# Forget attention: one inverse per query applied to the head's context instead of to every row of probabilities

## The reference

```python
sf = jnp.einsum('bqhd,bkhd->bhqk', qf, fk) * (FOX_HEAD_DIM ** -0.5)
sf = sf + cq[..., :, None] - cum_k[..., None, :]       # running sums of log forget gates
pf = jax.nn.softmax(jnp.where(causal, sf, NEG), axis=-1)
of = jnp.einsum('bhqk,bkhd->bqhd', pf, fv)
...
x = x + rmsnorm(concat([od, of]) @ w_out, ln_attn_post)
```

## Time and profile before

| | |
|---|---|
| median of 3 runs | 1392.2 us (1389.93 to 1393.25) |
| the profiled execution's own time | 1387.27 us |
| its span, first to last instruction | 1385.3 us |
| TensorE, weight load, VectorE, ScalarE busy | 1316.9, 1109.3, 784.4, 555.7 us |
| forget attention | 890.2 to 985.0 us of the span |
| mean granted TensorE clock | 0.983 |

### The profile page before, as it was taken

One profiled execution on the slowest core, in us unless ns is written; L12 is line 12 of the kernel. 1 busy time (PEld: TensorE's weight loads), 2 busy tenths in 40 slices (PEclk: granted clock), 3 DMA queues, 4 the chain that ended last, 5 costly groups with the idle time before them and its releaser, 6 DMA issues.

```text
span 1385.3 us, 17842 instructions
## 1 busy us (share of the span) xinstructions
PE 1316.9 (95%) x6548; PEld 1109.3 (80%) x6548; DVE 784.4 (57%) x1298; ACT 555.7 (40%) x914; POOL 44.9 (3%) x47
## 2 busy tenths in 40 slices
PE   7998879999999999999999999999899999999996
PEld 6877767789888888888777887878798788888886
DVE  5776767556644544222675797586685632355434
ACT  5645545534323223322454654555552322223221
POOL 3000000000000000000021000010000000000002
PEclk9999989999999999999999999999999999999999
DMA  5220110321232233333223232330211232222322
GB/s 177 92 92 16 54 46 16 99 69 61 92 100 97 91 97 113 109 106 106 91 91 107 91 99 84 92 92 31 92 62 61 92 107 91 91 97 100 106 92 76
DMA packets 37101, 120.46 MB, mean 87 GB/s; under 512 B 4508, under 2 KB 6556, under 8 KB 37040
## 3 DMA queue, kind: packets, MB, share of 16 engines
q1 hardware_dynamic: 36464, 117.98, 26.2%
q0 software_dynamic: 576, 1.65, 0.4%
HBM read 112.27 MB, written 2.11 MB: 83 GB/s over the span
## 4 chain that ended last, share of the span: by engine, by line
PE 77%; DVE 14%; ACT 4%; issue 3%; DMA 1%; POOL 0%; POOLq 0%; ACTq 0%; DVEq 0%; SPq 0%
PE bank L779 24%; PE bank L781 24%; PE bank L780 24%; DVE w_lo L1863 3%; DVE tiles L1863 2%; DVE tiles L1866 2%; DVE arena L1863 2%; DVE probsT L1863 1%; PE bank L923 1%; ACT w_hi L1327 1%; PE bank L885 1%; PE bank L876 1%; DVE arena L1866 1%; DVE negmax L2071 1%; ACT arena L1348 1%
## 5 line engine op out<-in xcount | busy, mean ns | idle before, releaser
L1863 DVE TENSOR_TENSOR w_lo<-raw_slab,w_hi 128x1024 fp32r<-128x1024 f32 x199 | 244.3, 1227 | 295.1 <-ACT w_hi L1327 279.7
L779 PE MATMUL bank<-u_hi,w_hi 128*128 128x512 f32 x852 | 337.8, 396 | 14.8 <-DVE tiles L1863 3.8
L781 PE MATMUL bank<-u_hi,w_lo 128*128 128x512 f32 x852 | 334.3, 392 | 0.0
L780 PE MATMUL bank<-u_lo,w_hi 128*128 128x512 f32 x852 | 334.2, 392 | 0.0
L1327 ACT ACTIVATE w_hi<-raw_slab 128x1024 fp32r<-128x1024 f32 x189 | 199.2, 1054 | 183.7 <-PE bank L781 179.9
L779 PE MATMUL bank<-arena,w_hi 128*128 128x512 f32 (+1 forms) x672 | 253.8, 378 | 9.7 <-DVE w_lo L1863 4.9
L780 PE MATMUL bank<-arena,w_hi 128*128 128x512 f32 (+1 forms) x672 | 251.8, 375 | 0.0
L781 PE MATMUL bank<-arena,w_lo 128*128 128x512 f32 (+1 forms) x672 | 251.8, 375 | 0.0
L779 PEld LDWEIGHTS bank<-u_hi,w_hi 128*128 128x128 f32 x852 | 161.2, 189 | 51.7 <-DVE tiles L1863 5.1
L781 PEld LDWEIGHTS bank<-u_hi,w_lo 128*128 128x128 f32 x852 | 161.3, 189 | 34.3
L780 PEld LDWEIGHTS bank<-u_lo,w_hi 128*128 128x128 f32 x852 | 161.4, 189 | 31.8
(11 more groups left out here) (221 smaller groups left out, 1564.7 us busy)
## 6 DMA issues: line engine op xcount, KB each, us to landing
raw_slab<-in_stream SPq DMA_DIRECT2D x207, 512.0 KB, 3.4
arena<-arena SPq DMA_DIRECT2D x32, 128.0 KB, 2.3
residual<-in_xT SPq DMA_DIRECT2D x8, 256.0 KB, 7.8
out_hT<-residual SPq DMA_DIRECT2D x16, 128.0 KB, 1.7
arena<-forget_rows SPq DMA_DIRECT2D x8, 128.0 KB, 2.3
tiles<-in_pT POOLq DMA_DIRECT2D x2, 256.0 KB, 3.0
tiles<-bias_rows POOLq DMA_DIRECT2D x1, 512.0 KB, 3.9
tiles<-in_positions POOLq DMA_DIRECT2D x1, 256.0 KB, 3.5
```

What stands on the lines that cost most here:

```text
L779: pe.matmul(o, ws[0], xs[0], start=first, stop=False)
L780: pe.matmul(o, ws[0], xs[1], start=False, stop=False)
L781: return pe.matmul(o, ws[1], xs[0], start=False, stop=last)
L1863: return nc.vector.tensor_tensor(o, a, b, op)
```

## The change

In forget attention alone, the exponentials go into the transpositions as they are. VectorE takes one inverse of the four row sums of a head at once (`fox_inverse`, at its step 4h+5). TensorE spreads these 512 inverses over the partitions, four 128x128 matmuls against the identity into bank 6 (`fox_factor`, at the end of step 4h+6), and ScalarE copies the head's 64 rows of them to a tile (step 4h+7). When the context is complete, VectorE multiplies it with that tile in place (end of step 4h+9), ScalarE copies the high half from the tile (end of its step 4h+9), and VectorE makes the low half (end of step 4h+10; for the last head in the same step). Bank 6 holds factors, so contexts have bank 5 alone: the next head's context may begin when the product has been made (`fox_scaled`).

```diff
+LAG_FACTOR = LAG_HEAD - 3
-CTX_BANKS = {"ml": (5,), "mla": (5, 6), "df": (5,), "fx": (5, 6)}
+CTX_BANKS = {"ml": (5,), "mla": (5, 6), "df": (5,), "fx": (5,)}
 # plan_psum
+        if a == "fx":
+            for h in range(FX_H):
+                use(("factor", h), 6, (sem.fox_factor, h + 1), (sem.fox_kept, h + 1))
-                free = {"ml": ..., "df": (sem.ctx_scaled, u // ST + 1)}
+                free = {"ml": ..., "df": (sem.ctx_scaled, u // ST + 1), "fx": (sem.fox_scaled, u // ST + 1)}
 # TensorE, attention
-                        pe.wait_ge(sem.probs_ready, UNIT0[a] + v + 1)
+                        if a == "fx":
+                            pe.wait_ge(sem.exp_done, EXP0["fx"] + v + 1)
+                        else:
+                            pe.wait_ge(sem.probs_ready, UNIT0[a] + v + 1)
...
+                    if a == "fx" and at_head("fx", step, LAG_FACTOR) is not None:
+                        fox_factor(at_head("fx", step, LAG_FACTOR))
+            def fox_factor(h):
+                o, e = claim(("factor", h)), EXP0["fx"] + h * ST
+                pe.wait_ge(sem.fox_inverse, h + 1)
+                for i in range(ST):
+                    last = pe.matmul(o[:, i * P:(i + 1) * P], rowinv[:, e + i:e + i + 1].to_broadcast([P, P]), ident, start=True, stop=True)
+                last.then_inc(sem.fox_factor, 1)
 # ScalarE
-            attention("fx", softmax_exp("fx"), plain_head("fx", fx_rows), fx_filled)
+            def fox_head(step):
+                h = at_head("fx", step, LAG_FACTOR + 1)
+                if h is not None:
+                    r, tile = fx_rows(h)
+                    if h:
+                        act.wait_ge(sem.mix_lo, HEAD0["fx"] + h)
+                    nc.scalar.activation(tiles[r, TMP + 1], full(act, ("factor", h))[r, :], ACT.Copy).then_inc(sem.fox_kept, 1)
+                h = at_head("fx", step, LAG_HEAD)
+                if h is not None:
+                    r, tile = fx_rows(h)
+                    act.wait_ge(sem.fox_scaled, h + 1)
+                    nc.scalar.activation(arena[r, MIX_HI + tile], tiles[r, TMP + 1], ACT.Copy).then_inc(sem.mix_hi, 1)
+            attention("fx", softmax_exp("fx"), fox_head, fx_filled)
 # VectorE
+            def fox_inverse(step, units):
+                v = step - LAG_NORM
+                if 0 <= v < units and v % ST == ST - 1:
+                    e = EXP0["fx"] + v + 1 - ST
+                    dve.wait_ge(sem.exp_done, e + ST)
+                    nc.vector.reciprocal(rowinv[:, e:e + ST], rowsum[:, e:e + ST]).then_inc(sem.fox_inverse, 1)
+            def fox_head(step):
+                h = at_head("fx", step, LAG_HEAD)
+                if h is not None:
+                    r, _ = fx_rows(h)
+                    o = full(dve, ("ctx", "fx", h))
+                    dve.wait_ge(sem.fox_kept, h + 1)
+                    tt(tiles[r, TMP + 1], o[r, :], tiles[r, TMP + 1], ALU.mult).then_inc(sem.fox_scaled, 1)
+                if h != FX_H - 1:
+                    h = at_head("fx", step, LAG_HEAD + 1)
+                if h is not None:
+                    r, tile = fx_rows(h)
+                    mix_low("fx", h, r, tile, tiles[r, TMP + 1])
-            attention("fx", softmax("fx", one_softmax("fx")), row_maxima("fx"), plain_head("fx", fx_rows), fx_taken, fx_split)
+            attention("fx", fox_inverse, row_maxima("fx"), fox_head, fx_taken, fx_split)
```

More of the change, by code:

```diff
@@ L312, in attention @@
                 n = HEAD0[a] + u // ST
-                free = {"ml": (sem.sq_done, SQ0.get(f"ml{u // ST}", 0) + 1), "df": (sem.ctx_scaled, u // ST + 1)}
+                free = {"ml": (sem.sq_done, SQ0.get(f"ml{u // ST}", 0) + 1), "df": (sem.ctx_scaled, u // ST + 1), "fx": (sem.fox_scaled, u // ST + 1)}
                 use(("ctx", a, u // ST), CTX_BANKS[a][u // ST % len(CTX_BANKS[a])], (sem.ctx_ready, (UNIT0[a] + u + 1) // 2), free.get(a, (sem.mix_lo, n + 1)))
@@ L516, in __init__ @@
         self.fox_query = new("fox_query")
+        self.fox_inverse = new("fox_inverse")
+        self.fox_factor = new("fox_factor")
+        self.fox_kept = new("fox_kept")
+        self.fox_scaled = new("fox_scaled")
 def build(nc, xT, pT_in, pos_in, cols_in, square_in, onehot_in, relb_in, stream, out):
```

## The result

The changed kernel takes 1395.13 us (median of 7 runs, 1392.46 to 1397.67) against 1389.93 for the kernel before in the same 7 rounds (1388.40 to 1393.25): a ratio of 1.0040, 95% interval 1.0027 to 1.0052, so 3.8 to 7.2 us slower. Forecast were +4.9 us and 1397.1; the kernel before itself came out 2.3 us under the 1392.2 that the forecast started from, so the difference is what to compare. The profiled execution took 1397.67 us, the slowest of its seven, with a span of 1395.9.

The account below looks back on a forecast made before the run. TensorE's work and its standstills bound the kernel. Terms -1.1 +3.0 -0.5 +1.8 -0.6 +0.75 gave +3.4 us, with 1.5 for the clock +4.9: 1392.2 to 1397.1 us, range 1392.0 to 1400.0.

Parts of the forecast that it names:

- up to step 9: Before head 0's context: waits for scaled rows shrink by 1.1, small ones by 0.5, spread adds 0.45; -1.1 us.
- head 0, with the clock: Step 9 and behind: new stall, head 1's spread, one old wait gone, +3.0 us; lower clock behind it, +1.5.
- head 2: The chain after its last maximum takes 6.4 us instead of 5.5, with spread and product wait inside it; +0.9.
- The new wait: Head 1's first product of probabilities and values waits for head 0's context product, behind fq3's split; a stall of +3.2 us.
- The clock: Behind the new stall TensorE's clock falls to about 0.5 for one 3.4 us stretch; +1.5 us, bounds 0 and 4.5.
- The spreads: TensorE's four spreads a head take 0.45 us; seven of eight lie on its path, +3.2 us in all.
- The waits behind VectorE: Heads' TensorE waits on VectorE's product, low halves and splits; for heads 2 and 5, a 6.4 us chain, +1.8 for both.
- The end: After the last context the product precedes both halves, lengthening TensorE's 1.41 us wait by 0.75; the last spread is free.
- Rival 1: Forget attention: the clock holds, all else as forecast; +3.4 us, 1395.6; chance 0.20.
- rival 2: New stalls in forget attention come to 2 or 3 us, the clock stays; 0 to +2, say 1393; chance 0.20.
- Rival 4: ScalarE stands at each head's end for VectorE's product, every head paying 1 us more; +8 to +10, 1401; chance 0.07.
- Rival 3: Transpositions bound by scaling alone, context free in time, idle ahead of the end goes; -4.7 us, 1387.5; chance 0.05.

Follow-up runs that it names:

- e1_product_first: The changed kernel with VectorE's product of context and factors moved ahead to the place of the inverse; 1388.01 us, ratio 0.9987 to the kernel before.
- e2_one_bank_alone: The kernel before with forget attention's contexts in bank 5 alone, rows still scaled, no spreads, no product; ratio 1.0021 to the kernel before.
- e3_busy_in_wait: The changed kernel with 13 unread matmuls just ahead of TensorE's wait for head 0's product; ratio 1.0020 to the kernel before.
- e4_spreads_twice: The changed kernel with each head's four spreads made twice into the same bank; ratio 1.0072 to the kernel before.
- e5_one_spread: e1_product_first with the four spreads for head 0 only, one matmul of one column for each other head; ratio 0.9992 to the kernel before.
- e6_diagonal: e1_product_first with the spread made as one float32 product of ones with a diagonal from GpSimd; ratio 1.0012 to the kernel before.
- e9_diagonal_in_halves: e1_product_first with the last head's product and halves in two parts, and factors from two GpSimd diagonals in float32r; ratio 0.9996 to the kernel before.

## Why the prediction was right, and where its sizes were off

The forecast's sum against the two profiled executions, each part measured between the starts of the same transpositions:

| part | forecast | measured |
|---|---|---|
| up to step 9 | -1.1 | 26.15 to 25.37: -0.8 |
| head 0, with the clock | +3.0 +1.5 | 9.16 to 15.39: +6.2 |
| head 1 | -0.5 | 9.53 to 8.88: -0.65 |
| head 2 | +0.9 | 11.41 to 11.81: +0.4 |
| head 3 | 0 | 8.37 to 8.61: +0.2 |
| head 4 | -0.6 | 12.22 to 11.95: -0.3 |
| head 5 | +0.9 | 8.11 to 9.39: +1.3 |
| end | +0.75 | 9.84 to 10.61: +0.8 |
| sum | +4.9 | 94.79 to 102.01: +7.2 |

- **The new wait** was the decisive term and held: 3.2 forecast, 3.05 recorded (3.2 with the 0.15 that the forecast adds for modelled ends), the same chain; e1_product_first and e2_one_bank_alone show it from both sides.
- **The clock** fell as forecast, but for 6.8 us, not one stretch of 3.4, and cost 2.9 instead of 1.5 (e3_busy_in_wait). It was inside the bounds; the value taken was the low one. e2_one_bank_alone and e4_spreads_twice have the same wait and show one stretch each, and no run here tells what makes it one or two. The price of one was right, its working less so: the nine matmuls counted in 3.4 us are eight from start to start (870.05 to 873.44), which take 1.9 us at full clock, a loss of 1.5 and not 1.2.
- **The spreads** were mis-sized. The step "the trace has the same 32 for the differential heads" failed: those 32 records belong to four heads, 16 spreads in the code of two float32 records each. A head costs 0.89, not 0.45, so the seven are 6.2 us long and not 3.2. That their whole length adds to the time is not shown: a second set adds 5.2 for these seven (e4_spreads_twice), and leaving most of them out of e1_product_first takes off 1.4 (e5_one_spread).
- **The waits behind VectorE** were reckoned too high. The chain behind head 2's maximum runs as described (6.1 us, 948.84 to 954.94, where 6.4 were reckoned), but TensorE with its longer spreads now arrives when it does, so it shows no wait there. Without the clock the stretch grew by 4.3 us where 3.4 were forecast, though the spreads are 3.0 longer than their term: some 2.1 of that was taken up by time counted as waits. That the sum still came near the median is partly such luck: 4.9 against 5.6 by the ratio, but 7.2 in the stretch.
- **The end** held to 0.1 us: 2.17 against 1.41 before, and the last head's spread free.
- Rival 1 (the clock holds) is out by the 0.50 behind the wait, and rival 2 by the wait's length. Rival 4's wider jam didn't come: the waits for the product at the other heads are 0.24, 0.24 and 0.38 us.
- Rival 3's condition, the context free in time, was met in e1_product_first, and the gain was 0.6 us in the stretch instead of 4.7: the spreads are 3 us longer than it allowed, and waits for the low halves in probsT stayed (0.46 and 0.34). Without most of the spreads these waits grow to 3.7 us in all (e5_one_spread), so cheaper spreads alone wouldn't have brought its time either.

## What to carry to other kernels

When a buffer is given up, look for the instruction that releases the one left and read what stands ahead of it in its engine's queue: here a 0.7 us product behind a projection's split cost some 6 us in the profiled execution (3.2 of wait, 2.9 of clock), and moving it forward made the whole change neutral. Taking work from an engine that isn't the bottleneck pays only where its queue ends a wait, and one must ask what else in the same queue ends that wait next (here the split that frees the transposition's bank). When a row of the trace is used as a price, count its records against the loops of the code, since one line of source may be two records.

## What the runs showed of the hardware

- A float32 matmul is two records here (8 for a head's four spreads), while a float32 transposition is one (L934: 1 to 4 records for 1 to 4 tiles). From start to start a float32 matmul of 128 columns takes 0.22 us, both records together; one of 512 columns takes 0.86, 0.43 a record (e6_diagonal); a float32r matmul of 512 columns takes 0.24. Four narrow float32 ones cost as much as one wide one.
- Standing still for 3.05 us, amid full work on both sides, brought a granted clock of 0.50 in all three profiled executions that have this wait (the changed kernel, e2_one_bank_alone, e4_spreads_twice), for 6.8, 3.4 and 3.4 us; the 6.8 cost 2.9 us. In e3_busy_in_wait, with matmuls that nobody reads in the wait, it stayed at 1.00.
- At the end of the attention waits of 1.41 to 2.17 us were followed by a low clock in some profiled executions (0.74 or 0.53 in the 6.6 us behind, six of eleven) and not in others. At the lower clock a float32r matmul of 512 columns takes 0.43 us from start to start in place of 0.24, so 3.4 us of it cost some 1.5.
- GpSimd's 128x512 product took 1.04 us (mean of 8 in e6_diagonal) and 1.12 in pairs. VectorE's operations with two operands in SBUF took longer where they ran beside one: slab splits of 1.98 and 1.88 us in place of 1.22, and a head's low half of 1.20 (e6_diagonal) and 1.09 and 1.33 (e9_diagonal_in_halves) in place of 0.69. Those that read a PSUM bank kept their time (0.55 for 384 columns, beside a product or not). GpSimd's own pairs grew in two cases, from 2.16 to 3.02 and 2.49 us, both beside such an operation. Work given to an idle engine isn't free for that reason; this is read from the traces, and no run was made to part the two.
